# A pooled half with buffers of its own: turned, summed and multiplied earlier in a 256-token two-block transformer kernel

## The chip, the cores and the metric

The kernel runs on one core of a Trainium2 chip. The metric is the time of one execution on the device, in microseconds (us). The kernel before takes 3283.55 us (median of 3 runs, 3282.36 to 3285.16).

## What is computed

The program runs two transformer blocks over 256 tokens of width 2048, all in float32. The first is a mixer of three attention branches followed by an MLP; the second has two layers, of which the first mixes with a sparse attention and a multiscale pool (`mixer_ab`). The change touches the first projection of `mixer_ab` and the pool behind it:

```python
z = h @ w_in                                   # 256 x 2048 times 2048 x 5200
q, k, v, qi, ki, wi, u = split(z)              # u: the last 1024 columns
# multiscale_pool(u, w, b, scale): four groups of 256 channels, windows 2, 4, 8, 16
for g, win in enumerate((2, 4, 8, 16)):
    c = cumsum(u[:, g], axis=tokens)
    out[g] = (c - shift(c, win)) / min(t + 1, win) - u[:, g]
mixed = einsum('btgc,gcd->btgd', out, w) + b   # one 256 x 256 product for each group
return mixed * scale
```

## The kernel before, in words

**Weights.** Every weight matrix streams through a ring of eight slots (`raw`). SyncE's queue issues one load for each chunk of 256 rows by up to 512 columns and waits for `chunk_used`, the count of chunks that TensorE has finished, before a slot is loaded again. ScalarE copies a chunk to a rounded high part (`split_hi`, line 290), VectorE takes the difference as the low part (`split_lo`, line 301), and TensorE multiplies high by high, low by high and high by low (lines 315 to 317, `mm_chunk`): 12 matmuls a chunk. A block is eight chunks that accumulate into one PSUM bank pair; ScalarE then evicts it (`scaled`, line 1430), once all eight chunks are used. All engines run their own lists in order, written out by hand; they meet only at semaphores.

**The order of the splits.** For each block ScalarE splits chunks 6 and 7 of the block itself and the first chunks of the next (slots 6 to 11 of the count), then evicts the block, and only then splits two more (12 and 13). VectorE follows the same count, 6 to 13, each behind ScalarE's half.

**The projection of `mixer_ab`** has eleven blocks (`AB_BLOCKS`): blocks 0 to 2 are 368 columns wide and hold ki, wi and u; blocks 3 and 4 hold qi; blocks 5 to 10 hold q, k and v. At the end of the first block's MLP the residual rows are scaled by GpSimd (`xres`, line 933) and turned by TensorE into the left operand `l_both`, 512 columns at a time; the last of these four turns stands inside block 0 of the projection (`turn`, line 410), after its chunk 1. The turned rows feed chunks 6 and 7.

**The pool** takes u in two halves of 512 columns (b = 0: windows 2 and 4; b = 1: windows 8 and 16). For each half:
- TensorE turns the rows (`turn`) into the PSUM view `tp4`: half 0 after chunk 3 of block 3, half 1 after chunk 3 of block 4. Half 1 needs `lhs_ready`, which VectorE raises at the start of `pool_sums(0)`.
- ScalarE copies them to the SBUF buffer `pu` (`pool_in`, line 1571).
- VectorE sums by doubling, between `pu`, `pa` and `pb` (`pool_sums`, `doubled`, line 2059), then forms the means (`pool_means`, `pooled`, lines 2063 to 2068) and raises `pool_dve`.
- TensorE multiplies by the pool weights, 16 matmuls (`pool_product`, line 1157), into `pool_out`. The pool weights lie in slots 0 and 1 of the ring, unsplit.
- VectorE adds the bias and scales (`pool_scaled`, line 2092), ScalarE takes the high part (`pool_hi`, line 1576), VectorE the low one (`pool_lo`, line 2098), both into `m_hi` and `m_lo`.

`pu`, `pa`, `pb` and `pool_out` exist once, so half 1 is copied into `pu` only when product 0 has read it. VectorE does `pool_sums(0)` and `pool_means(0)` after block 3's splits. The sums of half 1 stand in VectorE's list for block 5, behind `pool_scaled(0)`, `pool_lo(0)` and one split. Product 0 stands on TensorE ahead of block 5, product 1 inside block 5 after its chunk 4. SyncE's queue loads the last two chunks of block 5 only when product 0 and product 1 have read slots 0 and 1 (`pool_pe`). Inside block 6 TensorE begins the indexer (`index_step`, line 1172); its step 0 waits for `pool_dve` at 6, which is the end of `pool_lo(1)`.

Of the kernel before, what the change touches and what calls it, by code (L numbers as in the profile page):

```python
# [19 lines left out]
ALU = mybir.AluOpType  # L20
# [4 lines left out]
TOK = 256  # L25
# [93 lines left out]
def build_program(nc, d):  # L119

    with ExitStack() as ctx:
# [524 lines left out]

        PAD = 16
        pu, pa, pb = [view(late, 1088 * j, 4, PAD + TOK) for j in range(3)]
        pool_out = ps[:, 6:8, :].rearrange("p a (b c) -> p (a b) c", b=2)
        inv_head = view(late, 3264, 4, PAD)  # L650

# [226 lines left out]
        def _(pool):  # L878
# [77 lines left out]

            pool.wait_ge(merged, 13)
            nc.gpsimd.memset(late[:, 0:3264], 0.0).then_inc(pool_seq, 1)
            pool.dma_start(inv_head.rearrange("p a b -> p (a b)"), d["inv_head"].to_broadcast([P, 64])).then_inc(aux_in, 16)
            pool.wait_ge(pool_dve, 4)  # L960
            pool.dma_start(lim, d["chunk_lim"]).then_inc(aux_in, 16)
            pool_attend(pool, ud, N_D, TD)
            load_mixer_end(0)
# [14 lines left out]
        def _(pe):  # L978
# [167 lines left out]
            mlp_group(Q_MLP + 24, U_MLP + 24, 12, last=True)  # L1146
            def pool_product(b):

                pe.wait_ge(pool_dve, 1 + 3 * b)
                pe.wait_ge(raw_in[b], 16 * (Q_AB + AB_POOL + 1))  # L1150
                if b == 1:
                    pe.wait_ge(pool_dve, 2)
                pw = raw[:, b, :].rearrange("p (k c) -> p k c", k=4)
                for j in range(4):
                    o = pool_out[:, j, :]
                    for c in range(2):
                        m = nc.tensor.matmul(o, pw[:, 2 * (j // 2) + c, P * (j % 2):P * (j % 2 + 1)],
                                             pu[:, 2 * (j // 2) + c, PAD:],
                                             start=c == 0, stop=c == 1)
                    if (b, j) == (0, 0):  # L1160
                        m.then_inc(chunk_used, 2)
                m.then_inc(pool_pe, 1)
# [26 lines left out]
            for b, (c, w) in enumerate(AB_BLOCKS):  # L1189
                def each(c, b=b):  # L1190

                    if (b, c) == (0, 1):
                        turn(pe, T_X1 + 3, xres[:, :, 3 * BW:4 * BW], (merged, 13))
                    if (b, c) == (3, 3):
                        turn(pe, T_PU, zab[:, :, AB_U:AB_U + BW], (acc_free, U_AB + 3))
                    if (b, c) == (4, 3):
                        turn(pe, T_PU + 1, zab[:, :, AB_U + BW:AB_U + 2 * BW], (acc_free, U_AB + 3))
                    if (b, c) == (AB_POOL, 4):
                        pool_product(1)
                    p = 8 * (b - AB_POOL - 1) + c - 1  # L1200
                    if 0 <= p <= IDX_HEADS // 2:
                        index_step(p)

                if b == AB_POOL:
                    pe.wait_ge(lo_done, 8 * (Q_AB + b) + 2)
                    pool_product(0)
                mm_block(pe, Q_AB + b, U_AB + b, b % 2, lh, w=w, k0=0 if b < AB_POOL else O2,
                         need=(lhs_ready, T_X1) if b == 0 else None, each=each, rows=b == len(AB_BLOCKS) - 1)

# [189 lines left out]
        def _(act):  # L1399
# [165 lines left out]
            act.wait_ge(stat_v, 8)  # L1565
            def pool_in(b):

                act.wait_ge(pool_seq, 1)
                act.wait_ge(tp_done, T_PU + b + 1)
                wait(act, pool_pe, b)  # L1570
                nc.scalar.activation(pu[:, :, PAD:], tp4, ACT.Copy).then_inc(thi_done, 1)

            def pool_hi(b):

                act.wait_ge(pool_dve, 2 + 3 * b)
                nc.scalar.activation(mh[0][:, 8 + 4 * b:12 + 4 * b, :], pb[:, :, PAD:], ACT.Copy).then_inc(pool_act, 1)

            def index_step(p):
                if p == 0:
# [13 lines left out]
            for b, (c, w) in enumerate(AB_BLOCKS):  # L1593
                o, q = (0 if b < AB_POOL else O2), Q_AB + b
                if b == AB_POOL:
                    pool_in(1)
                    pool_hi(0)
                    split_hi(act, q, (6, 7))
                if b == AB_POOL + 2:
                    index_step(8)  # L1600
                for x in range(6):
                    if b == AB_POOL and x == 5:
                        pool_hi(1)
                    if b == AB_POOL + 1:
                        index_step(x)
                    split_hi(act, q, (o + 6 + x,))
                scaled(0, 0, 8 * q + o + 8, lambda tt: zab[:, tt, c:c + w], ST["rstd12"], b % 2, w=w,
                       row0=R_AB if b == len(AB_BLOCKS) - 1 else None)
                if b < 10:
                    for x in range(2):  # L1610
                        if b == AB_POOL + 1:
                            index_step(6 + x)
                        split_hi(act, q, (o + 12 + x,))
                if b == 3:
                    pool_in(0)
# [223 lines left out]
        def _(dve):  # L1839
# [216 lines left out]
            S = slice(PAD, PAD + TOK)  # L2056

            def doubled(dst, src, n, tl):
                chain(nc.vector.tensor_tensor(dst[:, tl:, S], src[:, tl:, S], src[:, tl:, PAD - n:PAD + TOK - n], ALU.add))

            def pooled(sums, g):
                x = slice(2 * (g % 2), 2 * (g % 2) + 2)
                chain(nc.vector.scalar_tensor_tensor(pu[:, x, 2 * PAD:], sums[:, x, 2 * PAD:], 1.0 / POOL_WINDOWS[g],
                                                     pu[:, x, 2 * PAD:], ALU.mult, ALU.subtract))
                h = slice(PAD, 2 * PAD)
                chain(nc.vector.tensor_tensor(sums[:, x, h], sums[:, x, h],
                                              inv_head[:, g:g + 1, :].to_broadcast([P, 2, PAD]), ALU.mult))
                return nc.vector.tensor_tensor(pu[:, x, h], sums[:, x, h], pu[:, x, h], ALU.subtract)


            def pool_sums(b):
                dve.wait_ge(aux_in, 16)
                dve.wait_ge(thi_done, T_PU + b + 1)
                dve.sem_inc(lhs_ready, 1)
                doubled(pa, pu, 1, 0)
                if b == 0:
                    doubled(pb, pa, 2, 2)
                else:
                    doubled(pb, pa, 2, 0)
                    doubled(pa, pb, 4, 0)  # L2080

            def pool_means(b):
                if b == 1:
                    doubled(pb, pa, 8, 2)
                pooled(pa, 2 * b)
                pooled(pb, 2 * b + 1).then_inc(pool_dve, 1)

            def pool_scaled(b):
                dve.wait_ge(pool_pe, b + 1)
                for j in range(4):  # L2090
                    c = 4 * b + j
                    i = nc.vector.tensor_scalar(pb[:, j, PAD:], pool_out[:, j, :], pk[:, PACK["pool_b"] + c:PACK["pool_b"] + c + 1],
                                                pk[:, PACK["pool_scale"] + c:PACK["pool_scale"] + c + 1], ALU.add, ALU.mult)
                i.then_inc(pool_dve, 1)

            def pool_lo(b):
                dve.wait_ge(pool_act, b + 1)
                nc.vector.tensor_tensor(mh[1][:, 8 + 4 * b:12 + 4 * b, :], pb[:, :, PAD:],
                                        mh[0][:, 8 + 4 * b:12 + 4 * b, :].bitcast(F32), ALU.subtract).then_inc(pool_dve, 1)


# [27 lines left out]
            for b in range(1, 11):  # L2129
                o, q = (0 if b < AB_POOL else O2), Q_AB + b  # L2130
                if b == AB_POOL:
                    pool_scaled(0)
                    pool_lo(0)
                    split_lo(dve, q, (6,))
                    pool_sums(1)
                    split_lo(dve, q, (7,))
                    pool_means(1)
                if b == AB_POOL + 2:
                    index_step(8)
                for x in range(8 if b < 10 else 6):  # L2140
                    if b == AB_POOL and x == 4:
                        pool_scaled(1)
                    if b == AB_POOL and x == 6:
                        pool_lo(1)
                    if b == AB_POOL + 1:
                        index_step(x)
                    split_lo(dve, q, (o + 6 + x,))
                    if b == AB_POOL + 3:
                        select(x)
                if b == 3:  # L2150
                    index_rows()
                    pool_sums(0)
                    pool_means(0)

            def store_m(used, u, par, b, add):

# [377 lines left out]
```

## Time and profile before

| | before |
|---|---|
| median of 3 runs | 3283.55 us |
| the profiled execution, time | 3280.64 us |
| the profiled execution, span | 3278.8 us |
| TensorE busy | 3257.3 us (99%) |
| VectorE busy | 1998.4 us (61%) |
| ScalarE busy | 1618.2 us (49%) |
| GpSimd busy | 181.8 us (6%) |
| HBM read | 603.22 MB, 185 GB/s over the span |

The profiled execution took 3280.64 us, 1.8 us more than its span and 2.9 us less than the median of the runs. TensorE is busy in all but 21.5 us of the span. Busy time counts a matmul from its start to its modelled end, so consecutive matmuls overlap: a 512-column matmul is shown 0.39 us long, and the next starts 0.23 us after it. What a step costs TensorE is read from the starts, not from the durations.

### The profile page before, as it was taken

How to read it: one execution, taken by the hardware profiler on the slowest of the kernel's cores; microseconds unless marked ns; L12 is line 12 of the kernel's file. 1: busy time of each engine (PE TensorE's matmuls, PEld its weight loads, DVE VectorE, ACT ScalarE, POOL GpSimd, SP SyncE). 2: the span in 40 equal slices, each digit the busy share in tenths (PEclk: the TensorE clock that was granted, in tenths of full speed). 3: DMA queues.
4: the chain of work that ended last, by engine and by line, in shares of the span. 5: the costliest groups of instructions: out<-in, count | busy, mean ns of one | idle time of the engine just before them, and what ended most of it. 6: DMA issues, size and time to landing. Idle time of an engine off the chain costs nothing.

```text
span 3278.8 us, 42815 instructions
## 1 busy us (share of the span) xinstructions
PE 3257.3 (99%) x16478; PEld 2755.4 (84%) x16478; DVE 1998.4 (61%) x2497; ACT 1618.2 (49%) x2264; POOL 181.8 (6%) x194
## 2 busy tenths in 40 slices
PE   9999999999999999999999999999999999999999
PEld 7888888888888888888978888888888878888887
DVE  6466555555555545555565677756766657774775
ACT  6455544444443444344544565545555746554453
POOL 0022200010000000000000200000010020000000
PEclk9999999999999999999999999999999999999999
DMA  7845666666666666666656566666656546666665
GB/s 251 240 132 155 172 181 193 193 186 199 187 192 192 187 193 189 193 187 177 195 163 187 168 192 188 191 192 186 186 181 194 171 142 190 191 190 191 186 187 159
DMA packets 323927, 608.89 MB, mean 186 GB/s; under 512 B 19468, under 2 KB 46424, under 8 KB 323120
## 3 DMA queue, kind: packets, MB, share of 16 engines
q1 hardware_dynamic: 320256, 594.05, 60.8%
q0 software_dynamic: 3504, 12.52, 1.5%
q8 instruction: 116, 1.90, 0.2%
q14 instruction: 51, 0.42, 0.0%
HBM read 603.22 MB, written 3.28 MB: 185 GB/s over the span
## 4 chain that ended last, share of the span: by engine, by line
PE 95%; DVE 2%; ACT 1%; DMA 1%; issue 0%; POOL 0%; SPq 0%; DVEq 0%; ACTq 0%
PE ps L347 21%; PE ps L315 18%; PE ps L317 18%; PE ps L316 18%; PE ps L348 11%; PE ps L333 1%; PE ps L335 1%; PE ps L334 1%; PE ps L513 1%; DVE w_lo L301 1%; DMA raw<-w_in 1%; PE ps L537 1%; PE ps L410 1%; ACT w_hi L290 0%; PE ps L502 0%; PE ps L539 0%
## 5 line engine op out<-in xcount | busy, mean ns | idle before, releaser
L301 DVE TENSOR_TENSOR w_lo<-raw,w_hi 128x1024 fp32r<-128x1024 f32 (+3 forms) x1138 | 1370.1, 1239 | 614.9 <-ACT w_hi L290 596.6
L290 ACT ACTIVATE w_hi<-raw 128x1024 fp32r<-128x1024 f32 (+3 forms) x1138 | 1149.3, 1042 | 713.7 <-DMA raw<-w_mlp_out 143.5
L347 PE MATMUL ps<-l_both,w_hi 128*128 128x512 f32 x2944 | 1032.2, 396 | 0.6 <-issue 0.6
L348 PE MATMUL ps<-l_both,w_lo 128*128 128x256 f32 x2944 | 822.5, 279 | 0.0
L347 PEld LDWEIGHTS ps<-l_both,w_hi 128*128 128x128 f32 x2944 | 552.5, 188 | 133.4 <-issue 1.1
L315 PE MATMUL ps<-w_hi,m_hi 128*128 128x512 f32 (+1 forms) x1476 | 572.1, 388 | 1.0 <-ACT l_rows L1430 1.0
L317 PE MATMUL ps<-w_hi,m_lo 128*128 128x512 f32 (+1 forms) x1476 | 569.6, 386 | 0.0
L316 PE MATMUL ps<-w_lo,m_hi 128*128 128x512 f32 (+1 forms) x1476 | 569.2, 386 | 0.0
L348 PEld LDWEIGHTS ps<-l_both,w_lo 128*128 128x128 f32 x2944 | 555.0, 189 | 0.3
L315 PE MATMUL ps<-w_hi,l_both 128*128 128x512 f32 (+3 forms) x1260 | 483.5, 384 | 4.1 <-DVE w_lo L301 3.4
L317 PE MATMUL ps<-w_hi,l_both 128*128 128x512 f32 (+3 forms) x1260 | 476.4, 378 | 0.0
L316 PE MATMUL ps<-w_lo,l_both 128*128 128x512 f32 (+3 forms) x1260 | 476.0, 378 | 0.0
L315 PEld LDWEIGHTS ps<-w_hi,m_hi 128*128 128x128 f32 x1476 | 277.3, 188 | 56.7 <-ACT l_rows L1430 1.3
L317 PEld LDWEIGHTS ps<-w_hi,m_lo 128*128 128x128 f32 x1476 | 277.2, 188 | 55.8
L316 PEld LDWEIGHTS ps<-w_lo,m_hi 128*128 128x128 f32 x1476 | 277.4, 188 | 54.8
L315 PEld LDWEIGHTS ps<-w_hi,l_both 128*128 128x128 f32 x1260 | 236.7, 188 | 48.3 <-DVE w_lo L301 4.2
L317 PEld LDWEIGHTS ps<-w_hi,l_both 128*128 128x128 f32 x1260 | 236.6, 188 | 42.6
L316 PEld LDWEIGHTS ps<-w_lo,l_both 128*128 128x128 f32 x1260 | 236.9, 188 | 39.4
L2299 DVE TENSOR_TENSOR main<-ps,main 128x1024 f32<-128x1024 f32 x30 | 36.7, 1225 | 154.9 <-ACT main L1696 154.9
L1696 ACT ACTIVATE main<-ps 128x1024 f32<-128x1024 f32 x30 | 30.8, 1027 | 177.7 <-PE ps L348 177.7
L1430 ACT ACTIVATE main<-ps,stats 128x512 f32<-128x512 f32 (+3 forms) x78 | 48.5, 666 | 139.0 <-PE ps L317 126.2
L2310 DVE SCALAR_TENSOR_TENSOR main<-main 128x255 f32<-128x255 f32 (+1 forms) x240 | 99.9, 478 | 2.9 <-ACT main L1711 1.1
(360 smaller groups left out, 2234.3 us busy)
## 6 DMA issues: line engine op xcount, KB each, us to landing
raw<-ffn_up SPq DMA_DIRECT2D x256, 512.0 KB, 3.7
raw<-w_in SPq DMA_DIRECT2D x176, 512.0 KB, 3.7
raw<-w_mlp_in SPq DMA_DIRECT2D x128, 512.0 KB, 3.7
raw<-w_mlp_out SPq DMA_DIRECT2D x128, 512.0 KB, 4.5
raw<-ffn_down SPq DMA_DIRECT2D x128, 512.0 KB, 3.9
raw<-ab_w_in SPq DMA_DIRECT2D x64, 512.0 KB, 3.6
raw<-w_branch SPq DMA_DIRECT2D x48, 512.0 KB, 3.9
raw<-cd_w_in SPq DMA_DIRECT2D x40, 512.0 KB, 3.8
```

The source lines that it names most:

```text
L290: nc.scalar.activation(w_hi[:, k % RING, 0:n], raw[:, k % RING, 0:n], ACT.Copy).then_inc(hi_done, 1)
L301: nc.vector.tensor_tensor(w_lo[:, k % RING, 0:n], raw[:, k % RING, 0:n], w_hi[:, k % RING, 0:n].bitcast(F32), ALU.subtract).then_inc(lo_do ...
L315: nc.tensor.matmul(o, xh, hi[:, j, :], start=first and j == 0, stop=False)
L316: nc.tensor.matmul(o, xh, lo[:, j, :], start=False, stop=False)
L317: m = nc.tensor.matmul(o, xl, hi[:, j, :], start=False, stop=last and j == len(kts) - 1)
L333: nc.tensor.matmul(o, xh, hi[:, j, :], start=first and j == 0, stop=False)
L334: nc.tensor.matmul(o, xh, lo[:, j, :], start=False, stop=False)
L347: nc.tensor.matmul(o, hi[:, j, cols], l_both[:, kt, :], start=first and j == 0, stop=False)
L348: m = nc.tensor.matmul(o[:, 0:TOK], lo[:, j, cols], lh[0][:, kt, :], start=False, stop=last and j == len(kts) - 1)
L1430: i = nc.scalar.activation(dst(tt), acc(par, w)[:, tt, :], func, scale=scale[:, tt:tt + 1])
L2299: nc.vector.tensor_tensor(z4, ps[:, 4 * val:4 * val + 4, 0:TOK], z4, ALU.add).then_inc(acc_free, 1)
L2310: i = nc.vector.scalar_tensor_tensor(dst[:, x, n:], z[:, x, 0:TOK - n], fcw[:, 2 - n, k:k + 1], dst[:, x, n:], ALU.mult, ALU.add)
```

## The change

The second half gets buffers of its own, `pu1` and `pb1`, laid over the start of `m_hi` and `m_lo`, which nobody else uses at that time; GpSimd clears their 16 columns of padding with two more memsets. Product 1 writes to `tp4` instead of `pool_out`.

- TensorE: the turn of half 1 moves from after chunk 3 to after chunk 1 of block 4. Product 1 moves from after chunk 4 of block 5 to right behind product 0, ahead of block 5. The last turn of `xres` moves from after chunk 1 to after chunk 2 of block 0.
- ScalarE: `pool_in(1)` moves from the head of block 5's list into block 4's, after split 9. `pool_hi(1)` moves forward, between splits 6 and 7 of block 5.
- VectorE: `pool_sums(1)` and `pool_means(1)` move to the end of block 4's list, behind all eight of its splits. At the head of block 5 stand `pool_scaled(0)`, `pool_scaled(1)`, `pool_lo(0)`, split 6, `pool_lo(1)` and split 7.
- GpSimd: the load of `lim` waits for `pool_dve` at 2 instead of 4; the count now runs means 0, means 1, scaled 0, scaled 1, low 0, low 1.

SyncE's queue and the amount of arithmetic are unchanged.

```diff
+        pu1, pb1 = [view(m_rows[:, j], 0, 4, PAD + TOK) for j in range(2)]
@@ GpSimd
             nc.gpsimd.memset(late[:, 0:3264], 0.0).then_inc(pool_seq, 1)
+            nc.gpsimd.memset(pu1[:, :, 0:PAD], 0.0)
+            nc.gpsimd.memset(pb1[:, :, 0:PAD], 0.0).then_inc(pool_seq, 1)
-            pool.wait_ge(pool_dve, 4)
+            pool.wait_ge(pool_dve, 2)
@@ TensorE
-                pe.wait_ge(pool_dve, 1 + 3 * b)
+                pe.wait_ge(pool_dve, 1 + b)
-                if b == 1:
-                    pe.wait_ge(pool_dve, 2)
-                    o = pool_out[:, j, :]
+                    o = (pool_out, tp4)[b][:, j, :]
-                                             pu[:, 2 * (j // 2) + c, PAD:],
+                                             (pu, pu1)[b][:, 2 * (j // 2) + c, PAD:],
-                    if (b, c) == (0, 1):
+                    if (b, c) == (0, 2):
                         turn(pe, T_X1 + 3, xres[:, :, 3 * BW:4 * BW], (merged, 13))
-                    if (b, c) == (4, 3):
+                    if (b, c) == (4, 1):
                         turn(pe, T_PU + 1, zab[:, :, AB_U + BW:AB_U + 2 * BW], (acc_free, U_AB + 3))
-                    if (b, c) == (AB_POOL, 4):
-                        pool_product(1)
                 if b == AB_POOL:
                     pe.wait_ge(lo_done, 8 * (Q_AB + b) + 2)
                     pool_product(0)
+                    pool_product(1)
@@ ScalarE
-                act.wait_ge(pool_seq, 1)
+                act.wait_ge(pool_seq, 1 + b)
                 act.wait_ge(tp_done, T_PU + b + 1)
-                wait(act, pool_pe, b)
-                act.wait_ge(pool_dve, 2 + 3 * b)
+                act.wait_ge(pool_dve, 3 + b)
                 if b == AB_POOL:
-                    pool_in(1)
                     pool_hi(0)
-                    split_hi(act, q, (6, 7))
+                    split_hi(act, q, (6,))
+                    pool_hi(1)
+                    split_hi(act, q, (7,))
-                    if b == AB_POOL and x == 5:
-                        pool_hi(1)
                     split_hi(act, q, (o + 6 + x,))
+                    if (b, x) == (4, 3):
+                        pool_in(1)
@@ VectorE
                 if b == AB_POOL:
                     pool_scaled(0)
+                    pool_scaled(1)
                     pool_lo(0)
                     split_lo(dve, q, (6,))
-                    pool_sums(1)
+                    pool_lo(1)
                     split_lo(dve, q, (7,))
-                    pool_means(1)
-                    if b == AB_POOL and x == 4:
-                        pool_scaled(1)
-                    if b == AB_POOL and x == 6:
-                        pool_lo(1)
                 if b == 3:
                     index_rows()
                     pool_sums(0)
                     pool_means(0)
+                if b == 4:
+                    pool_sums(1)
+                    pool_means(1)
```

## Rows read from the trace of the kernel before

**Rows 1.** The page: the span, and the busy time of each engine.
```profile
span 3278.8 us, 42815 instructions
...
PE 3257.3 (99%) x16478; PEld 2755.4 (84%) x16478; DVE 1998.4 (61%) x2497; ACT 1618.2 (49%) x2264; POOL 181.8 (6%) x194
```

**Rows 2.** Timeline, TensorE, both products: start, us, line, operation, [idle before <- releaser].
```profile
1653.06 3.61 PE L1157 MATMUL ps<-late,raw 128*128 128x256 f32 x16
1656.32 0.58 PE L315 MATMUL ps<-w_hi,l_both 128*128 128x512 f32 x1
...
1669.89 0.39 PE L317 MATMUL ps<-w_hi,l_both 128*128 128x512 f32 x1
1670.89 3.72 PE L1157 MATMUL ps<-late,raw 128*128 128x256 f32 x16 [0.61 <-DVE late L2068]
1674.26 0.59 PE L315 MATMUL ps<-w_hi,l_both 128*128 128x512 f32 x1
```

**Rows 3.** Timeline, ScalarE, at the end of block 4: its eviction and two splits.
```profile
1653.25 1.26 ACT L1430 ACTIVATE main<-ps,stats 128x512 f32<-128x512 f32 x2 [7.11 <-PE ps L317]
1654.41 2.00 ACT L290 ACTIVATE w_hi<-raw 128x1024 fp32r<-128x1024 f32 x2
```

**Rows 4.** Timeline, VectorE, from the start of half 0's sums to half 1's low part.
```profile
1635.32 0.17 DVE L2053 TENSOR_SCALAR main<-main 128x32 f32<-128x32 f32 x1
...
1655.50 2.36 DVE L301 TENSOR_TENSOR w_lo<-raw,w_hi 128x1024 fp32r<-128x1024 f32 x2 [8.10 <-ACT w_hi L290]
1657.77 1.90 DVE L2092 TENSOR_SCALAR late<-ps,pk_sb 128x256 f32<-128x256 f32 x4
...
1663.08 3.74 DVE L2059 TENSOR_TENSOR late<-late 128x1024 f32<-128x1024 f32 x3
...
1667.99 0.69 DVE L2059 TENSOR_TENSOR late<-late 128x512 f32<-128x512 f32 x1
...
1670.65 0.19 DVE L2068 TENSOR_TENSOR late<-late 128x32 f32<-128x32 f32 x1
...
1688.45 1.22 DVE L2098 TENSOR_TENSOR m_lo<-late,m_hi 128x1024 fp32r<-128x1024 f32 x1
```

**Rows 5.** Timeline, TensorE: the last chunk of block 5, and the indexer's first transpose.
```profile
1680.76 0.50 PE L315 MATMUL ps<-w_hi,l_both 128*128 128x512 f32 x1 [0.66 <-DVE w_lo L301]
...
1689.77 0.41 PE L1172 MATMUL ps<-ident_sb,main 128*128 128x128 f32 x2 [0.55 <-issue]
```

**Rows 6.** Waits of SyncE's queue: waited for, us in total, times, longest.
```profile
SPq L269 <- PE ps L1157: 20.1, 2, 17.5
```

**Rows 7.** Timeline, TensorE, around the last turn of `xres` in block 0.
```profile
1560.83 0.33 PE L316 MATMUL ps<-w_lo,l_both 128*128 128x368 f32 x1
1561.00 0.33 PE L317 MATMUL ps<-w_hi,l_both 128*128 128x368 f32 x1
1562.63 1.09 PE L410 MATMUL ps<-ident_sb,xres 128*128 128x128 f32 x8 [1.29 <-POOL xres L933]
1563.47 0.41 PE L315 MATMUL ps<-w_hi,l_both 128*128 128x368 f32 x1
```

**Rows 8.** Timeline, VectorE: the splits of block 0's last chunks.
```profile
1569.56 5.10 DVE L301 TENSOR_TENSOR w_lo<-raw,w_hi 128x736 fp32r<-128x736 f32 x6 [0.89 <-ACT w_hi L290]
```

**Rows 9.** Timeline, GpSimd: the load of `lim`.
```profile
1671.13 0.54 POOL L961 DMA_DIRECT2D main<-chunk_lim x1 [105.13 <-DVE late L2068]
```

**Rows 10.** Timeline, TensorE: its first transposes of the run and its last matmul.
```profile
2.57 2.40 PE L984 MATMUL ps<-ident_sb 128*128 128x128 f32 x10 [2.57 <-DMA ident_sb<-ident]
5.70 1.97 PE L410 MATMUL ps<-ident_sb,xres 128*128 128x128 f32 x8 [0.74 <-DMA xres<-x]
7.46 2.71 PE L984 MATMUL ps<-ident_sb 128*128 128x128 f32 x14
...
3270.60 0.39 PE L335 MATMUL ps<-w_hi,m_lo 128*128 128x512 f32 x1
```

**Rows 11.** Windows, tail: length, PE, PEld, DVE, ACT, POOL busy, granted clock, DMA.
```profile
3276.00:3277.00 1.00, 0.00 (x0) 0.00 (x0) 0.00 (x0) 0.00 (x0) 0.00 (x0) 0.55 0.98 389
```

More of the change, by code:

```diff
@@ L1566, in pool_in @@
             def pool_in(b):
-                act.wait_ge(pool_seq, 1)
+                act.wait_ge(pool_seq, 1 + b)
                 act.wait_ge(tp_done, T_PU + b + 1)
-                wait(act, pool_pe, b)
-                nc.scalar.activation(pu[:, :, PAD:], tp4, ACT.Copy).then_inc(thi_done, 1)
+                nc.scalar.activation((pu, pu1)[b][:, :, PAD:], tp4, ACT.Copy).then_inc(thi_done, 1)
             def pool_hi(b):
-                act.wait_ge(pool_dve, 2 + 3 * b)
-                nc.scalar.activation(mh[0][:, 8 + 4 * b:12 + 4 * b, :], pb[:, :, PAD:], ACT.Copy).then_inc(pool_act, 1)
+                act.wait_ge(pool_dve, 3 + b)
+                nc.scalar.activation(mh[0][:, 8 + 4 * b:12 + 4 * b, :], (pb, pb1)[b][:, :, PAD:], ACT.Copy).then_inc(pool_act, 1)
             def index_step(p):
@@ L2061, in pooled @@
             def pooled(sums, g):
-                x = slice(2 * (g % 2), 2 * (g % 2) + 2)
-                chain(nc.vector.scalar_tensor_tensor(pu[:, x, 2 * PAD:], sums[:, x, 2 * PAD:], 1.0 / POOL_WINDOWS[g],
-                                                     pu[:, x, 2 * PAD:], ALU.mult, ALU.subtract))
+                x, u = slice(2 * (g % 2), 2 * (g % 2) + 2), (pu, pu1)[g // 2]
+                chain(nc.vector.scalar_tensor_tensor(u[:, x, 2 * PAD:], sums[:, x, 2 * PAD:], 1.0 / POOL_WINDOWS[g],
+                                                     u[:, x, 2 * PAD:], ALU.mult, ALU.subtract))
                 h = slice(PAD, 2 * PAD)
@@ L2067, in pooled @@
                                               inv_head[:, g:g + 1, :].to_broadcast([P, 2, PAD]), ALU.mult))
-                return nc.vector.tensor_tensor(pu[:, x, h], sums[:, x, h], pu[:, x, h], ALU.subtract)
+                return nc.vector.tensor_tensor(u[:, x, h], sums[:, x, h], u[:, x, h], ALU.subtract)
             def pool_sums(b):
@@ L2074, in pool_sums @@
                 dve.sem_inc(lhs_ready, 1)
-                doubled(pa, pu, 1, 0)
                 if b == 0:
+                    doubled(pa, pu, 1, 0)
                     doubled(pb, pa, 2, 2)
                 else:
-                    doubled(pb, pa, 2, 0)
-                    doubled(pa, pb, 4, 0)
+                    doubled(pa, pu1, 1, 0)
+                    doubled(pb1, pa, 2, 0)
+                    doubled(pa, pb1, 4, 0)
             def pool_means(b):
                 if b == 1:
-                    doubled(pb, pa, 8, 2)
+                    doubled(pb1, pa, 8, 2)
                 pooled(pa, 2 * b)
-                pooled(pb, 2 * b + 1).then_inc(pool_dve, 1)
+                pooled((pb, pb1)[b], 2 * b + 1).then_inc(pool_dve, 1)
             def pool_scaled(b):
@@ L2091, in pool_scaled @@
                     c = 4 * b + j
-                    i = nc.vector.tensor_scalar(pb[:, j, PAD:], pool_out[:, j, :], pk[:, PACK["pool_b"] + c:PACK["pool_b"] + c + 1],
+                    i = nc.vector.tensor_scalar((pb, pb1)[b][:, j, PAD:], (pool_out, tp4)[b][:, j, :], pk[:, PACK["pool_b"] + c:PACK["pool_b"] + c + 1],
                                                 pk[:, PACK["pool_scale"] + c:PACK["pool_scale"] + c + 1], ALU.add, ALU.mult)
@@ L2097, in pool_lo @@
                 dve.wait_ge(pool_act, b + 1)
-                nc.vector.tensor_tensor(mh[1][:, 8 + 4 * b:12 + 4 * b, :], pb[:, :, PAD:],
+                nc.vector.tensor_tensor(mh[1][:, 8 + 4 * b:12 + 4 * b, :], (pb, pb1)[b][:, :, PAD:],
                                         mh[0][:, 8 + 4 * b:12 + 4 * b, :].bitcast(F32), ALU.subtract).then_inc(pool_dve, 1)
```

## The prediction

> **What bounds the kernel now.** I read the page first. TensorE is busy 3257.3 of 3278.8 us [rows 1], so it has 21.5 us of idle time in all; VectorE, ScalarE and GpSimd have plenty. Nothing that saves work elsewhere can show, and a wait added on TensorE shows in full, because no slack follows it. So the second view is TensorE's timeline around the pool, where each step is priced by the time from its start to the next start; the third is the timelines of ScalarE and VectorE, to see when each would hand TensorE what the new order asks of it.
>
> The reader should see three small losses that the change aims at. Product 1 was due at 1669.89 + 0.23 = 1670.12 and started at 1670.89, held by the last step of the means [rows 2]: 0.77. The last chunk of block 5 waited 0.66 for its low part [rows 5]; its load stood behind `pool_pe`, for which SyncE's queue waited up to 17.5 us [rows 6]. The indexer's first transpose waited 0.55, up to 1689.77 [rows 5], just when `pool_lo(1)` ends, 1688.45 + 1.22 = 1689.67 [rows 4]. A fourth lies in block 0: the turn of `xres` waited 1.29 for GpSimd [rows 7].
>
> **Part 1, the sums of half 1 at the end of block 4's list.** This decides. VectorE reaches them after splits 12 and 13. Those follow ScalarE's splits, which stand behind the eviction of block 4, and that starts only at 1653.25, when block 4's last chunk is done [rows 3]. So the two low parts run at 1655.50 and end where the next instruction starts, 1657.77 [rows 4]. The 8.10 us for which VectorE idles before them are not used: its list has the sums behind them. In the trace the sums and means of half 1 took 3.74 us (three doublings from 1663.08, to 1666.82), then one split that is not part of them, then 2.85 us (1667.99 to 1670.65 + 0.19) [rows 4]: 6.6 us. After the change they start at 1657.77 and end at about 1664.4. No operation is added: buffers and shapes have the same sizes.
>
> **Part 2, product 1 ahead of block 5.** TensorE now asks for the means as soon as product 0 has been issued, at 1656.32 [rows 2]. The semaphore comes at 1664.4, and the handover takes 0.05 (1670.84 to 1670.89) [rows 2, 4]. So TensorE waits about 1664.44 - 1656.32 = 8.1 us. Behind the wait, on its own list, stands the whole of block 5, whose weights are ready: nothing can fill the gap. Product 1 itself costs the same in both places (3.37 from 1670.89 to 1674.26, against 3.26 for product 0 [rows 2]). The start of product 1 moves 14.6 us forward, while its input moves only 6.4 us forward.
>
> **Part 3, what is removed.** The 0.77 ahead of product 1, the 0.66 in the last chunk of block 5 and the 0.55 at the indexer go: the two loads are then released together, right after the products, five chunks before they are needed, and `pool_lo(1)` ends before TensorE is through block 5's chunk 3. Each interruption also costs a seam, since the matmul after it is stretched (0.59 against 0.39 [rows 2]); three seams are 0.6. Together -2.6 us.
>
> **Part 4, the turn of `xres` one chunk on.** A matmul of 368 columns starts 0.17 after the last one [rows 7], a chunk of twelve takes 2.02. Chunk 2 then runs from 1561.17 to 1563.2, past the moment at which GpSimd is ready, so the 1.29 goes at first. But the turn starts 0.56 later (1563.2 against 1562.63 [rows 7]), and the chain behind it (turned rows, squares, root, then the splits of chunks 6 and 7 on both engines) shifts with it. Before, chunk 6 began at 1563.47 + 4 x 2.02 = 1571.55, after its low part at 1569.56 + 5.10/6 = 1570.4 [rows 7, 8]. Now TensorE would be there at 1570.1, and the low part comes at 1571.0. The gain is 1571.55 - 1571.0, about -0.5; its bounds are 0 and -1.3.
>
> **Part 5, moves that I cost at nothing.** The turn of half 1 after chunk 1 of block 4: counted back from product 0 at 1653.06, six chunks of 2.72 and one turn of 0.84 give 1635.9, while VectorE raises `lhs_ready` right after 1635.32 + 0.17 = 1635.5 [rows 2, 4, 7]. It holds by 0.4 us; without that cover it is a wait of some tenths. `pool_in(1)` on ScalarE waits for the load of the pool weights to pass the width-0 splits, and has until 1657.8. The two memsets and the earlier load of `lim` lie in GpSimd's 105.13 us of idle time [rows 9]. `pool_scaled(0)` and `pool_hi(0)` come some 7 us later than before and splits 6 and 7 of block 5 with them: VectorE does scaled 0 until 1666.3, scaled 1 until about 1670, low 0 and split 6 until 1672.5, and TensorE needs split 6 four chunks after 1667.8, at 1678.7. The cover is 6 us.
>
> **Part 6, the clock.** No row of before shows TensorE waiting 8 us in the middle of the run. The nearest are at its ends. After the last matmul at 3270.60 + 0.39 [rows 10] the granted clock is 0.55 on average between 3276 and 3277 [rows 11], so it fell from 2.4 to 1.2 GHz about 5.1 us after that matmul's end. A wait of 8.1 us is longer than that. At the start of the run, after rest, eight transposes take 7.46 - 5.70 = 1.76 us [rows 10] against 1563.47 - 1562.63 = 0.84 [rows 7], twice as long; the thirty-two transposes of that stretch lose about 2.8 us (0.9 on the eight, 1.0 on the ten, 0.9 on the fourteen). So what follows the wait runs at half pace for a while. Its cost lies between 0 (the clock stays) and 3.3 (the sixteen matmuls of product 1 all take twice their 0.204), or 6.0 if block 5's first chunk is slow too (+2.7). I take 2.6, close to the start of the run.
>
> The Trainium skill speaks against this change: its page "TensorE: Matmul & The Clock Gate" (section "What's actually happening") says that the throttled clock is the default and that activity releases it, so an idle stretch would be paid for twice, once as waiting and once at half rate. The tail's clock here agrees; that the rate falls in mid-run no row of before shows. By the page the clock term stands; without it the sum is that of rival B.
>
> **The sum.** 8.1 + 2.6 - 2.6 - 0.5 = +7.6 us. Against the profiled execution that is 3280.64 + 7.6 = 3288.2; that execution was 2.9 us below the median of the runs, so I put the sum on the median: 3283.55 + 7.6 = 3291.2 us, 0.23% slower.
>
> **The rivals.**
> A, the forecast: TensorE waits and its clock falls. +7.6, own range +6.0 to +9.0 (3289.5 to 3292.5).
> B, the side that is not slower: TensorE waits for the means, but its clock holds at 2.4 GHz. Then 8.1 - 2.6 - 0.5 = +5.0, 3288.6 us, 0.15%: within what can be measured. The point is at a fall that costs less than 1.6 us, since 0.2% is 6.6 us. For it speaks that the trace grants 1.00 everywhere but in the tail, against it the 5.1 us there [rows 10, 11].
> C, the clock returns late, or a second wait follows in block 5: product 1 and the first chunk at half pace, 8.1 + 6.0 - 2.6 - 0.5 = +11.0, 3294.6 us.
> D, the change does as it says and half 1 is summed before TensorE asks for it. The sums would have to start by 1656.3 - 6.6 = 1649.7, within the 8.10 us of idle time before 1655.50 [rows 4]. Then no wait, and -2.6 - 0.5 = -3.1: 3280.4 us, also within 0.2%. The order of the lists speaks against it: ScalarE's eviction and two splits stand in front [rows 3].
>
> **How the numbers follow.** A 0.60, B 0.20, C 0.13, D 0.05, something unseen 0.02. A measurement of this kernel tells about 0.2% (6.6 us) from no change. A lies above that in about 17 of 20 cases, C always, B and D below it. Slower 0.69, same 0.28, faster 0.03. The range takes in B with half a microsecond below its sum and more than half of what lies between A and C: 3287.5 to 3294.0.
>
> **What would show each step.** Product 1 starts right behind product 0 in the list but some 8 us later in time, held by the last `pooled` step (line 2068's successor), and this is TensorE's longest wait. VectorE's sums of half 1 start at once behind the two splits after block 4's eviction. The granted clock shows 0.50 inside or after that wait, and product 1's matmuls start 0.4 apart instead of 0.2. The waits at block 5's last chunk and at the indexer are gone; SyncE's queue waits for `pool_pe` about half as long at most. In block 0 the turn waits for nobody and chunk 6 waits some 0.9 us for its low part. The prediction is wrong if the sums run in VectorE's idle time before the splits, if the clock holds, or if the removed waits come back in block 6.

## The result and the profile after

The changed kernel takes 3290.2 us (median of 14 runs, 3288.51 to 3293.94) against 3283.86 us for the kernel before in 14 runs beside it: 6.3 us more, ratio 1.0022 with a 95% interval of 1.0015 to 1.0029. It is slower, by about as much as was forecast. One execution of a variant below, "only the means late", took 6152.2 us at a mean granted clock of 0.84, and its ratio leaves that one out.

The page of the profiled execution, beside [rows 1]: the span is 8.8 us longer, and TensorE's busy time has hardly moved.

```profile
span 3287.6 us, 42816 instructions
...
PE 3259.1 (99%) x16478; PEld 2756.3 (84%) x16478; DVE 1999.0 (61%) x2497; ACT 1619.3 (49%) x2264; POOL 182.0 (6%) x196
```

TensorE's busy time grew by 1.8 us, so most of the time went into waits. The list of TensorE's waits over the whole run has a new longest one (waited for, us in total, times, longest):

```profile
PE ps L1158 <- DVE m_rows L2069: 7.8, 1, 7.8
PE ps L315 <- DVE w_lo L301: 3.2, 3, 1.7
PE ps L315 <- DVE l_both L435: 2.7, 1, 2.7
```

The first is product 1 behind the last step of the means. The third is in the first 12 us of the run, where the two programs are the same, and by the start of block 0 this profile is 2.1 us behind that of before, with nothing changed in between. Executions differ there by some us: block 0 of the projection starts anywhere between 1557.1 and 1562.5 us in the nine profiles of this study, with the same instructions in front of it on TensorE. Part of that is the clock: the two latest starts, 1561.91 and 1562.52 us, belong to the two executions in which the granted clock fell twice in the first 160 us (last section). The span of one profile is therefore a poor ruler for a change of this size. Below, two stretches inside a profile are used: from the start of block 0 to product 0 (**stretch P**), and from the start of block 0 to the indexer's first transpose (**stretch I**). Before, they are 1653.06 - 1557.15 = 95.91 and 1689.77 - 1557.15 = 132.62 us [rows 2, 5].

TensorE's timeline after, the lines that answer to [rows 2, 5, 7]: block 0's first matmul, the turn of `xres`, chunk 6 of block 0, both products, block 5's start, and the indexer.

```profile
1559.25 0.33 PE L315 MATMUL ps<-w_hi,l_both 128*128 128x368 f32 x1
...
1565.28 1.04 PE L410 MATMUL ps<-ident_sb,xres 128*128 128x128 f32 x8
...
1573.24 0.41 PE L315 MATMUL ps<-w_hi,l_both 128*128 128x368 f32 x1 [0.91 <-DVE w_lo L301]
...
1654.83 3.61 PE L1158 MATMUL ps<-late,raw 128*128 128x256 f32 x16
1666.23 5.25 PE L1158 MATMUL ps<-m_rows,raw 128*128 128x256 f32 x16 [7.79 <-DVE m_rows L2069]
1671.13 0.58 PE L315 MATMUL ps<-w_hi,l_both 128*128 128x512 f32 x1
...
1698.54 0.38 PE L1173 MATMUL ps<-ident_sb,main 128*128 128x128 f32 x2
```

Stretch P is 95.58 us (-0.33), stretch I is 139.29 us (+6.67). Product 1 was due at 1654.83 + 3.26 = 1658.09 and started at 1666.23, 8.14 later, and it took 1671.13 - 1666.23 = 4.90 instead of 3.37. The indexer and block 5's last chunk wait for nothing any more, and the turn of `xres` waits for nothing either, but chunk 6 waits 0.91.

ScalarE's timeline beside [rows 3], and VectorE's beside [rows 4], show where the means come from:

```profile
1655.03 1.27 ACT L1430 ACTIVATE main<-ps,stats 128x512 f32<-128x512 f32 x2 [6.25 <-PE ps L317]
1656.18 2.00 ACT L290 ACTIVATE w_hi<-raw 128x1024 fp32r<-128x1024 f32 x2
```
```profile
1657.27 2.36 DVE L301 TENSOR_TENSOR w_lo<-raw,w_hi 128x1024 fp32r<-128x1024 f32 x2 [7.24 <-ACT w_hi L290]
1659.55 1.22 DVE L2060 TENSOR_TENSOR late<-m_rows 128x1024 f32<-128x1024 f32 x1
...
1665.98 0.19 DVE L2069 TENSOR_TENSOR m_rows<-m_rows 128x32 f32<-128x32 f32 x1
...
1675.60 1.23 DVE L2100 TENSOR_TENSOR m_lo<-m_rows,m_hi 128x1024 fp32r<-128x1024 f32 x1
```

Eviction, two high parts, two low parts, then the sums: 1659.55 to 1666.17, 6.62 us, with 7.24 us of idle time just before. `pool_lo(1)` now ends at 1676.83, more than 20 us before the indexer asks for it.

The granted clock in windows of 1 us (length, busy of PE, PEld, DVE, ACT and POOL, clock, DMA; a clock of 1.00 is 2.4 GHz, 0.50 is 1.2): it fell inside the wait, at about 1662.5, and rose again at about 1669.4, 3.1 us after product 1 began.

```profile
1661.00:1662.00 1.00, 0.00 (x0) 0.00 (x0) 1.00 (x1) 0.00 (x0) 0.00 (x0) 1.00 0.37 139
1662.00:1663.00 1.00, 0.00 (x0) 0.00 (x0) 0.96 (x2) 0.00 (x0) 0.00 (x0) 0.77 0.00 0
1663.00:1664.00 1.00, 0.00 (x0) 0.00 (x0) 0.97 (x2) 0.00 (x0) 0.00 (x0) 0.50 0.00 0
...
1669.00:1670.00 1.00, 1.00 (x5) 0.86 (x4) 0.00 (x0) 1.00 (x2) 0.00 (x0) 0.82 0.00 0
1670.00:1671.00 1.00, 1.00 (x6) 0.87 (x6) 0.00 (x0) 0.03 (x1) 0.00 (x0) 1.00 0.00 0
```

### The profile page after: what moved, and what is told of

It is laid out like the page before. It is cut to its first block, busy times and chain, and to the rows that moved or that the text cites. A ratio compares the mean times of both kernels' runs of the same rounds, so it can differ in the third digit from the quotient of the medians.

```text
span 3287.6 us, 42816 instructions
## 1 busy us (share of the span) xinstructions
PE 3259.1 (99%) x16478; PEld 2756.3 (84%) x16478; DVE 1999.0 (61%) x2497; ACT 1619.3 (49%) x2264; POOL 182.0 (6%) x196
## 4 chain that ended last, share of the span: by engine, by line
PE 96%; DVE 2%; ACT 1%; DMA 1%; issue 0%; SPq 0%; DVEq 0%; ACTq 0%
PE ps L347 21%; PE ps L315 18%; PE ps L317 18%; PE ps L316 18%; PE ps L348 11%; PE ps L333 1%; PE ps L335 1%; PE ps L334 1%; PE ps L513 1%; DVE w_lo L301 1%; DMA raw<-w_in 1%; PE ps L537 1%; PE ps L410 1%; ACT w_hi L290 0%; PE ps L502 0%; PE ps L539 0%
```

## The experiments

The theory to be tested: the loss is the wait for means that stand behind ScalarE's eviction in the hand-written lists, and the half clock that the wait leaves behind; the removed waits gave back some 2.6 us. The rivals: the new buffers or the PSUM view make product 1 slow by themselves; something other than the sums ends the wait; the turn's move was worth its whole 1.3 us. Diffs are against the changed kernel unless said otherwise.

**The sums put before the splits.**

```diff
                     split_lo(dve, q, (o + 6 + x,))
+                    if (b, x) == (4, 3):
+                        pool_sums(1)
+                        pool_means(1)
...
-                if b == 4:
-                    pool_sums(1)
-                    pool_means(1)
```

> The changed kernel, with VectorE's sums and means of half 1 behind its split 9 of block 4 instead of behind split 13. Theory (TensorE's loss is the wait for means that stand behind ScalarE's eviction in the lists): the means are ready by 1652, product 1 follows product 0 without a gap, 16 matmuls in 3.3 us at a granted clock of 1.00, and of the +6.3 us against before remain -0.3 (turn) and -2.6 (removed waits and seams): 3281.0 us, ratio 0.9991. Rival (the second half's own buffers or the PSUM view tp4 make product 1 slow, 4.9 us in the changed kernel): the 7.8 us wait goes, but product 1 still takes 4.9 us, 3282.5 us.

Measured: 3280.7 us, ratio 0.9988 (0.9979 to 0.9997). TensorE's and VectorE's timelines:

```profile
1661.53 3.62 PE L1158 MATMUL ps<-m_rows,raw 128*128 128x256 f32 x16
1664.79 0.58 PE L315 MATMUL ps<-w_hi,l_both 128*128 128x512 f32 x1
```
```profile
1647.23 1.23 DVE L2060 TENSOR_TENSOR late<-m_rows 128x1024 f32<-128x1024 f32 x1 [0.42 <-DVEq L299]
...
1653.68 0.19 DVE L2069 TENSOR_TENSOR m_rows<-m_rows 128x32 f32<-128x32 f32 x1
1653.79 2.35 DVE L301 TENSOR_TENSOR w_lo<-raw,w_hi 128x1024 fp32r<-128x1024 f32 x2
```

In this profile product 0 starts at 1658.07, the means are ready at 1653.87, and product 1 starts 0.2 us after it was due, with no wait, and takes 3.26 us from the same buffers. Stretch I is 129.68 us, 2.94 less than before and 9.61 less than in the changed kernel. Where the sums stand is the whole loss, the wait and the clock that falls in it; the new buffers cost nothing, and the rest of the change is worth about 3 us.

**TensorE kept busy while it waits.**

```diff
                     pool_product(0)
+                    pe.wait_ge(thi_done, T_PU + 2)
+                    for j in range(70):
+                        nc.tensor.transpose(tp4[:, j % 4, 0:P], ident[:], ident[:])
                     pool_product(1)
```

> The changed kernel, with 70 transposes of the identity into tp4 between product 0 and product 1, so that TensorE is busy for about 7.4 of the 8.1 us for which it waits for the means; product 1 overwrites them. Theory (product 1 was slow because the granted clock fell in the idle time): the clock stays at 1.00, product 1 starts at the same time and takes 3.3 to 3.4 us instead of 4.9, 1.5 us less than the changed kernel: 3288.7 us. Rival (it was slow for its buffers): product 1 again takes 4.9 us and the time is that of the changed kernel, 3290.2 us.

Measured: 3288.22 us, ratio 1.0015 (1.0006 to 1.0024), 2.0 us under the changed kernel. TensorE's timeline, and the granted clock over that stretch:

```profile
1658.05 7.80 PE L1208 MATMUL ps<-ident_sb 128*128 128x128 f32 x70
1666.00 3.72 PE L1158 MATMUL ps<-m_rows,raw 128*128 128x256 f32 x16
1669.37 0.58 PE L315 MATMUL ps<-w_hi,l_both 128*128 128x512 f32 x1
```
```profile
1658.00:1666.00 8.00, 7.85 (x71) 7.57 (x70) 7.73 (x13) 0.00 (x0) 0.00 (x0) 1.00 0.23 68
```

The clock stays at 1.00 and product 1 takes 3.37 us, though it starts no sooner. Stretch I is 137.76 us, 1.53 less than in the changed kernel: the 4.90 - 3.37 of product 1. That part was the clock. The other 5.14 us against before are the wait, less what the change saves. By the times the saving is 2.0 us, but the two intervals overlap, so they can't tell 2.0 from 1.5.

**The sums one step later.**

```diff
                     pool_scaled(0)
+                    pool_sums(1)
+                    pool_means(1)
                     pool_scaled(1)
...
-                if b == 4:
-                    pool_sums(1)
-                    pool_means(1)
```

The counts of `pool_dve` are changed to match.

> The changed kernel, with VectorE's sums and means of half 1 one step further back, behind pool_scaled(0). Theory (TensorE's wait is the arrival of the means, one to one): the wait grows by what pool_scaled(0) takes, 1.8 to 1.9 us, from 7.8 to 9.7 us, and product 1 starts that much later; the clock is low when the wait ends in both, so product 1 and what follows lose at most 3.4 us: 3292.1 us, up to 3294. Rival (something else ends the wait, and the sums only happen to end there): 3290.2 us.

Measured: 3291.97 us, ratio 1.0026 (1.0016 to 1.0035).

```profile
1666.11 5.30 PE L1158 MATMUL ps<-m_rows,raw 128*128 128x256 f32 x16 [9.60 <-DVE m_rows L2069]
1671.06 0.58 PE L315 MATMUL ps<-w_hi,l_both 128*128 128x512 f32 x1
```

The wait is 9.60 instead of 7.79, 1.81 more, and stretch I is 141.14, 1.85 more. The wait is the arrival of the means, one to one. The time is 1.8 us above that of the changed kernel, with intervals that overlap; the stretch is what decides. The half clock costs no more after 9.6 us than after 7.8: product 1 takes 4.95.

**Only the means late.**

```diff
+                    if (b, x) == (4, 3):
+                        pool_sums(1)
...
                 if b == 4:
-                    pool_sums(1)
                     pool_means(1)
```

> The changed kernel, with the sums of half 1 behind VectorE's split 9 of block 4, and only the means (2.9 us) left behind split 13, so that TensorE waits about half as long. Theory (arrival of the means, plus a clock that falls only in a long wait): the wait is 8.1 - 3.8 = 4.3 us, the stretch from the start of block 0 to the indexer's first transpose takes 132.6 + 4.3 - 2.9 = 134.0 us if the clock holds at 1.00, which is what I expect, and up to 135.5 if it falls: 3285.3 us, ratio 1.0004. Rival (any wait here costs the half rate afterwards): product 1 takes 4.9 us or more and the stretch 135.5 us or more.

Measured: 3286.12 us, ratio 1.0011 (1.0002 to 1.0019). TensorE's timeline and three windows of the granted clock:

```profile
1660.32 5.24 PE L1158 MATMUL ps<-m_rows,raw 128*128 128x256 f32 x16 [4.01 <-DVE m_rows L2069]
1665.20 0.58 PE L315 MATMUL ps<-w_hi,l_both 128*128 128x512 f32 x1
```
```profile
1659.00:1660.00 1.00, 0.00 (x0) 0.00 (x0) 0.93 (x4) 0.00 (x0) 0.00 (x0) 1.00 0.37 139
1660.00:1661.00 1.00, 0.68 (x2) 0.59 (x3) 0.97 (x4) 0.00 (x0) 0.44 (x1) 0.50 0.00 0
...
1663.00:1664.00 1.00, 1.00 (x5) 0.84 (x4) 0.00 (x0) 1.00 (x2) 0.00 (x0) 0.79 0.00 0
```

The wait came as reckoned, but not what I expected of the clock: it fell in a wait of 4.0 us too, just before product 1 began, which took 4.88 us. Stretch I is 135.51 us, as the rival had it. Half the wait did not halve the clock's price.

**The turn of `xres` put back.**

```diff
-                    if (b, c) == (0, 2):
+                    if (b, c) == (0, 1):
```

> The changed kernel, with the last turn of xres back behind chunk 1 of block 0. Theory: the 1.29 us wait for GpSimd returns, the 0.91 us wait for split 6 goes, and from the start of block 0 to product 0 it takes 0.3 to 0.4 us more: 3290.5 us. Rival (the turn's move was worth the whole 1.3 us): 3291.5 us.

Measured: 3291.03 us, ratio 1.0023 (1.0014 to 1.0033).

```profile
1567.39 1.10 PE L410 MATMUL ps<-ident_sb,xres 128*128 128x128 f32 x8 [1.29 <-POOL xres L934]
...
1669.26 6.76 PE L1158 MATMUL ps<-m_rows,raw 128*128 128x256 f32 x16 [7.79 <-DVE m_rows L2069]
1675.66 0.58 PE L315 MATMUL ps<-w_hi,l_both 128*128 128x512 f32 x1
```

The wait for GpSimd is back, and stretch P is 95.95 us (block 0 starts at 1561.91, product 0 at 1657.86), 0.37 more. Stretch I is 141.19, 1.90 more, but 1.50 of it is product 1, which took 6.40 us in this execution: the clock came back only 6.2 us after it began. The time lies between the 3290.5 of the theory and the 3291.5 of the rival and decides nothing; stretch P does.

```profile
1675.00:1676.00 1.00, 1.00 (x5) 0.86 (x4) 0.00 (x0) 0.00 (x0) 0.00 (x0) 0.78 0.00 0
```

**The turn moved alone**, in the kernel before.

```diff
-                    if (b, c) == (0, 1):
+                    if (b, c) == (0, 2):
```

> The kernel before, with nothing changed but the last turn of xres behind chunk 2 of block 0. Theory (the chain behind the turn sets chunk 6): the 1.29 us wait goes, a wait of 0.9 us for split 6 comes, and the stretch from the start of block 0 to product 0 takes 95.6 us instead of 95.9: 3283.5 us, not to be told from before. Rival (the wait for GpSimd was a loss of its own): 1.3 us less, 94.6 us and 3282.6 us.

Measured: 3283.56 us, ratio 1.0001 (0.9992 to 1.0009).

```profile
1565.22 1.04 PE L410 MATMUL ps<-ident_sb,xres 128*128 128x128 f32 x8
1573.17 0.41 PE L315 MATMUL ps<-w_hi,l_both 128*128 128x368 f32 x1 [0.90 <-DVE w_lo L301]
```

Stretch P is 95.57 us, 0.34 less than before. A wait of 1.29 us is gone and one of 0.90 has taken its place. Stretch I is only 0.18 us less, for the wait in block 5's last chunk is 0.84 here instead of 0.66.

**Splits 6 and 7 of block 0 first**, together with the early sums.

```diff
                         turn_hi(act, T_X1 + b, tiles(lh, 4 * b), gains("mix_pre")[:, 4 * b:4 * b + 4])
+                        if b == 3:
+                            split_hi(act, Q_AB, (6, 7))
                         squares(xres[:, :, BW * b:BW * (b + 1)], b, ssp2, junk_x)
...
-                for x in range(6):
+                for x in range(2 if b == 0 else 0, 6):
...
             mlp_group(Q_MLP + 24, U_MLP + 24, 12, last=True)
+            split_lo(dve, Q_AB, (6, 7))
             mean_square(32, ST["mean"], ssp)
...
-            split_lo(dve, Q_AB, range(6, 14))
+            split_lo(dve, Q_AB, range(8, 14))
```

> The kernel with the sums of half 1 behind split 9 (e_sums_early), and besides ScalarE splits chunks 6 and 7 of block 0 ahead of the last squares of xres, VectorE ahead of the mean and the root. Theory: chunk 6 of block 0 then waits for nothing, the stretch from the start of block 0 to product 0 falls from 95.6 to 94.6 or 94.7 us, and the one to the indexer's first transpose from 129.7 to 128.7: 3279.8 us, ratio 0.9987 to before. Rival (the chain only moves: the root comes 1.7 us later, and the eviction of block 0 behind it holds TensorE in block 2): no gain, 129.7 us.

Measured: 3278.5 us, ratio 0.9984 (0.9975 to 0.9993), and TensorE waits for nobody between 1500 and 1720 us.

```profile
1653.60 3.61 PE L1158 MATMUL ps<-late,raw 128*128 128x256 f32 x16
...
1687.72 0.38 PE L1173 MATMUL ps<-ident_sb,main 128*128 128x128 f32 x2
```

Block 0 starts at 1559.21, so stretch P is 94.39 us and stretch I 128.51 us, 1.17 less than with the early sums alone. This kernel beats both: it is 4.7 us under the kernel before in the runs beside it (3283.17 us), and, each set against the kernel before beside it, 11.0 us under the changed one. From the early sums alone the times can't tell it (the intervals overlap); the stretches can.

The last column is each median less that of the kernel before in the runs beside it (3283.86, 3283.92 or 3283.17 us); the other columns come from one profile each.

| kernel | stretch P | stretch I | wait for the means | product 1 | time, us | against before |
|---|---|---|---|---|---|---|
| before | 95.91 | 132.62 | 0.61 | 3.37 | 3283.86 | |
| changed | 95.58 | 139.29 | 7.79 | 4.90 | 3290.2 | +6.3 |
| sums before the splits | 95.55 | 129.68 | none | 3.26 | 3280.7 | -3.2 |
| kept busy | 95.55 | 137.76 | filled | 3.37 | 3288.22 | +4.3 |
| sums one step later | 95.56 | 141.14 | 9.60 | 4.95 | 3291.97 | +8.1 |
| only the means late | 95.57 | 135.51 | 4.01 | 4.88 | 3286.12 | +3.0 |
| turn put back | 95.95 | 141.19 | 7.79 | 6.40 | 3291.03 | +7.1 |
| turn moved alone | 95.57 | 132.44 | 0.61 | 3.37 | 3283.56 | +0.4 |
| splits 6 and 7 first | 94.39 | 128.51 | none | 3.27 | 3278.5 | -4.7 |

## Why the prediction was right, step by step

The forecast was +7.6 us. The medians give +6.3, and the stretch with the change in it +6.67 in one execution of each kernel. The parts, as measured below, add up: 8.14 (wait) + 1.53 (clock) - 2.58 (removed waits and seams) - 0.33 (turn) = +6.76 us.

- **The sums (part 1).** Forecast to take 6.6 us and to start right behind the two splits. They took 6.62 us there. Shown: moving them by one step moved the wait by 1.81 us, and moving them before the splits removed it.
- **The wait (part 2).** Forecast 8.1 us; product 1 started 8.14 us after it was due.
- **The removed waits (part 3).** Forecast -2.6 us. With the early sums, stretch I is 2.94 below before; 0.36 of that lies in stretch P, the rest is 2.58. All three waits are gone. SyncE's queue still waits for `pool_pe`, and this check was put too boldly: the longest wait fell from 17.5 [rows 6] to 12.6 us, not to half, because product 1 itself came so late.

```profile
SPq L269 <- PE ps L1158: 15.1, 2, 12.6
```

- **The turn of `xres` (part 4).** Forecast -0.5, with 0 and -1.3 as bounds; it measured -0.33 to -0.37 in stretch P. The mechanism was right, a 0.91 us wait for split 6 in place of the 1.29 us for GpSimd. The turn started 6.03 us into block 0 instead of 5.48, and the chain behind it moved by about as much (the low parts began 12.92 us into the block instead of 12.41); chunk 6 then began 13.99 us into the block, 0.14 later than I had reckoned (13.85). Splitting chunks 6 and 7 ahead of the root removed that wait, and 1.2 us with it.
- **Nothing for the rest (part 5).** The turn of half 1 after chunk 1, the two memsets (0.15 us each) and the earlier load of `lim` show no wait on TensorE in the profile after.
- **The clock (part 6).** This is the term that was mis-sized: 2.6 us forecast, 1.53 in the profile of the changed kernel, by which stretch I falls short of the forecast as well. It isn't a constant: 1.5 us in three executions and 3.0 in a fourth (product 1 in 4.90, 4.95, 4.88 and 6.40 us). How often either comes in the runs without a profile is not known. The forecast took its 2.6 from the thirty-two transposes at the start of the run; here the clock came back 3.1 us after product 1 began, and that was the whole loss. The 2.6 was a choice between bounds of 0 and 6.0, with no row of a wait in mid-run behind it: it is off by 1.1 us, and no other part by more than 0.2.
- **The rivals.** B (the clock holds) would have given +5.0; the kernel that was kept busy is that case, made on purpose, and its stretch I is +5.14 (+4.3 by the times). C (+11.0) did not occur in the changed kernel's profile: no second wait follows in block 5, and the clock was back before block 5 began. The late return that C speaks of was seen once, with the turn put back, and cost 3.0 us instead of C's 6.0. D (the sums are in time) is the kernel with the early sums: forecast -3.1, measured -3.2 by the times and -2.94 in the stretch.
- **The chances and the range.** Two of their sums don't come out. A in 17 of 20 cases and C always make 0.64 for slower, at most 0.66 with the unseen, not 0.69. And the range begins 1.1 us below B's 3288.6, not half a microsecond. Neither touches the forecast itself.

The Trainium skill's page "TensorE: Matmul & The Clock Gate" (section "What's actually happening") had the throttled clock as the default and activity as what releases it. The runs agree: 0.50 in four waits of 4.0 to 9.6 us, 1.00 where the same time was filled with transposes. The fall with TensorE busy throughout (last section) is left unexplained by both.

One thing stays open: why the clock came back 3.1 to 3.2 us after product 1 began in three executions and after 6.2 us in one. No run was made for it.

## What to carry to other kernels

When a consumer is moved forward in a hand-written order, compare how far it moves with how far its input moves: here product 1's place in TensorE's list came 14.9 us earlier after the start of block 0 (98.84 us instead of 113.74) and its input only 6.8 (106.92 instead of 113.69), and the difference is the wait. The input's time is set by whatever stands in front of its producer in that engine's list, here splits that hung on an eviction which begins only when the block is done; idle time just before them is of no use unless the step is written there. And a wait on TensorE can be paid twice, once as waiting and once at the half clock: each of the unfilled waits of 4.0 to 9.6 us here was.

## What the hardware showed that was not expected

- The clock fell in a wait of only 4.0 us. I had expected it to hold, since in the tail of the run it fell 5.1 us after the last matmul [rows 10, 11]. Counted from the modelled end of the last matmul, it fell after about 3.7 us there and with the turn put back, after 4.1 us in the changed kernel, and after 2.6 us with the sums one step later:

```profile
1659.00:1660.00 1.00, 0.00 (x0) 0.00 (x0) 1.00 (x3) 0.45 (x1) 0.00 (x0) 0.55 0.39 148
```

- Its price does not grow with the wait (1.5 us after 4.0, 7.8 and 9.6 us), but varies between executions, from 1.5 to 3.0 us.
- The granted clock also fell where TensorE waited for nothing, and no run explains it. In two of the nine profiles, the early sums and the turn put back, it was 0.50 for 3.4 us twice in the first 160 us. The second time came at the end of a wait of 2.1 or 2.4 us; the first time TensorE was busy throughout. With the early sums:

```profile
126.00:127.00 1.00, 1.00 (x6) 1.00 (x6) 0.81 (x3) 0.93 (x1) 0.85 (x1) 0.50 0.00 0
127.00:128.00 1.00, 1.00 (x7) 1.00 (x6) 0.84 (x1) 0.13 (x1) 0.00 (x0) 0.50 0.42 93
```

Just before, TensorE had run sixteen matmuls of 32 columns; in the other profiles the same ones passed at 1.00. Twice 3.4 us at half the rate is an estimated 3.4 us, about what these two executions are late by at block 0. So the clock can differ between two executions of one program far from any change, and a difference between two spans should be held against it first.
